# Expert down-projection weights loaded in 8 KB pieces, gate/up weight columns read with a stride of four

## The reference

```python
def swiglu(h, w_gu, w_down):
    g, u = jnp.split(h @ w_gu, 2, axis=-1)
    return (jax.nn.silu(g) * u) @ w_down

def moe_swiglu(h, router_w, router_b, w_gu, w_down):
    ...
    for e in range(N_EXPERTS):
        y = y + combine[..., e:e + 1] * swiglu(h, w_gu[e], w_down[e])
```

## Time and profile before

| | us |
|---|---|
| median of three runs (lowest, highest) | 1466.25 (1466.15, 1468.07) |
| the profiled execution, its own time | 1464.35 |
| its span in the profile | 1462.6 |

### The profile page before, as it was taken

One profiled execution on the slowest core, in us unless ns is written; L12 is line 12 of the kernel. 1 busy time (PEld: TensorE's weight loads), 2 busy tenths in 40 slices (PEclk: granted clock), 3 DMA queues, 4 the chain that ended last, 5 costly groups with the idle time before them and its releaser, 6 DMA issues.

```text
span 1462.6 us, 38889 instructions
## 1 busy us (share of the span) xinstructions
PE 1267.1 (87%) x15885; PEld 802.6 (55%) x15885; DVE 750.8 (51%) x1108; ACT 324.3 (22%) x706; POOL 42.0 (3%) x43
## 2 busy tenths in 40 slices
PE   3898998999987689979988997999899799889940
PEld 1458966888876655535544553555455355445520
DVE  0687736777754545534443543444455344435422
ACT  1105644333333311111111111111111111111110
POOL 1010000000010120000000000000000000000001
PEclk8899999999998699989999998999999899989975
DMA  9985021888898047999999999999999999999943
GB/s 339 392 329 194 2 87 32 287 291 297 298 387 327 1 165 268 393 394 375 395 393 395 395 393 394 396 394 393 395 395 393 394 379 395 393 395 395 393 160 108
DMA packets 199498, 460.71 MB, mean 315 GB/s; under 512 B 9584, under 2 KB 34848, under 8 KB 199328
## 3 DMA queue, kind: packets, MB, share of 16 engines
q1 hardware_dynamic: 185296, 403.79, 74.3%
q0 software_dynamic: 13984, 56.49, 10.4%
q10 hardware_dynamic: 192, 0.08, 0.0%
HBM read 456.66 MB, written 4.59 MB: 315 GB/s over the span
## 4 chain that ended last, share of the span: by engine, by line
issue 64%; PE 27%; DMA 4%; DVE 3%; ACT 1%; POOL 1%; POOLq 0%; SPq 0%; DVEq 0%; ACTq 0%
PE ps L801 4%; PE ps L629 3%; PE ps L757 3%; PE ps L758 3%; PE ps L759 3%; DMA ctx_tok<-in_ctx 2%; PE ps L747 2%; PE ps L689 2%; DMA ada<-in_ada_w 1%; PE ps L594 1%; PE ps L678 1%; PE ps L912 1%; PE ps L670 1%; PE ps L669 1%; PE ps L666 1%
## 5 line engine op out<-in xcount | busy, mean ns | idle before, releaser
L937 PE MATMUL ps<-w_gu,consts_sb 128*32 128x256 f32 x8960 | 539.6, 393 | 73.2 <-DMA w_gu<-in_moe_w_gu 71.4
L937 PEld LDWEIGHTS ps<-w_gu,consts_sb 128*32 128x32 f32 x8960 | 282.4, 112 | 278.0 <-DMA w_gu<-in_moe_w_gu 83.8
L1604 DVE COPY w_dn<-w_next 128x2048 f32<-128x2048 f32 x280 | 329.9, 1221 | 0.0
L949 PE MATMUL ps<-w_dn,consts_sb 128*32 128x256 f32 x4512 | 274.8, 384 | 1.6 <-DVE w_dn L1604 1.6
L949 PEld LDWEIGHTS ps<-w_dn,consts_sb 128*32 128x32 f32 x4512 | 149.6, 112 | 103.7 <-issue 10.6
L1596 DVE TENSOR_TENSOR consts_sb<-consts_sb,ps 128x128 f32<-128x128 f32 x140 | 40.4, 288 | 297.2 <-ACT consts_sb L1198 287.8
L1198 ACT ACTIVATE consts_sb<-ps 128x128 f32<-128x128 f32 x140 | 38.9, 278 | 567.9 <-PE ps L937 567.9
L1600 DVE TENSOR_TENSOR y_all<-y_all,ps 128x256 f32 x140 | 59.0, 421 | 177.8 <-PE ps L949 177.8
L1288 DVE SCALAR_TENSOR_TENSOR ada_acc<-ada,cols,ada_acc 128x512 f32<-128x512 f32 x140 | 105.0, 750 | 4.0
L1418 DVE TENSOR_TENSOR f_lo<-f_raw,f_hi 128x2048 fp32r<-128x2048 f32 x33 | 75.5, 2292 | 54.2 <-ACT f_hi L1085 52.7
L1085 ACT ACTIVATE f_hi<-f_raw 128x2048 fp32r<-128x2048 f32 x33 | 63.2, 1917 | 70.2 <-DMA f_raw<-in_ffn_w_gu 57.7
(11 more groups left out here) (218 smaller groups left out, 967.2 us busy)
## 6 DMA issues: line engine op xcount, KB each, us to landing
w_gu<-in_moe_w_gu SPq DMA_DIRECT2D x224, 1024.0 KB, 14.9
w_next<-in_moe_w_down SPq DMA_DIRECT2D x112, 1024.0 KB, 13.2
ada<-in_ada_w POOLq DMA_DIRECT2D x23, 2048.0 KB, 9.9
f_raw<-in_ffn_w_gu SPq DMA_DIRECT2D x44, 512.0 KB, 6.8
f_raw<-in_ffn_w_down SPq DMA_DIRECT2D x11, 1024.0 KB, 5.0
wqkv<-in_attn_w_qkv SPq DMA_DIRECT2D x3, 2048.0 KB, 19.4
wo_sb<-in_attn_w_o SPq DMA_DIRECT2D x1, 4096.0 KB, 23.8
y_rows<-y_all SPq DMA_DIRECT2D x80, 32.0 KB, 1.5
```

What stands on the lines that cost most here:

```text
L937: mm = pe.matmul(ps[UNIT * t:UNIT * t + UNIT, GU_BANK, 0:2 * W], x_cur[:, k, :], gate_up_columns(w_gu[x], half, kk, t), start=(k == 0), st ...
L949: mm = pe.matmul(ps[UNIT * t:UNIT * t + UNIT, Y_BANK, 0:OW], m_actT[:, q % QW, q // QW, :], w_dn[:, q, OW * t:OW * t + OW], start=(q == 0) ...
L1604: dve.tensor_copy(w_dn[:, 2 * half:2 * half + 2, :], w_next[:, y, 2 * half:2 * half + 2, :]).then_inc(s[f"d_copied{half}"], 1)
```

## The change

Each partition now holds four consecutive rows of the slice's down weights: `w_dn[p, q]` is row 4 p + q. The two rows that one transfer brings to a partition are then 8 KB in one piece. To match, column tile t takes every fourth gate and up column, starting at t: its moving operand is two runs of 128 elements that are 16 bytes apart from one to the next, where before they were adjacent. The results that leave tile t are the hidden values 4 c + t for c = 0 to 127, which after the transpose lie on partition c of chunk t.

```diff
-    mdn_v = moe_down[0].rearrange("e (q p) n -> e p q n", p=P)
+    mdn_v = moe_down[0].rearrange("e (s p q) n -> e s p q n", p=P, q=MS // P)
...
         def load_down(y, e, step):
 
             for half in range(2):
-                src = mdn_v[bass.ds(e, 1), :, bass.ds(step * (MS // P) + 2 * half, 2), :]
-                sp.dma_start(w_next[:, y, 2 * half:2 * half + 2], src.rearrange("e p k n -> p (e k) n")
+                src = mdn_v[bass.ds(e, 1), bass.ds(step, 1), :, 2 * half:2 * half + 2, :]
+                sp.dma_start(w_next[:, y, 2 * half:2 * half + 2], src.rearrange("e s p q n -> p (e s q) n")
                              ).then_inc(s[f"d_in{y}{half}"], 16)
...
     def gate_up_columns(w, half, kk, t):
-        return w[:, 2 * half:2 * half + 2, kk, W * t:W * t + W]
+        return w[:, 2 * half:2 * half + 2, kk, :].rearrange("p a (c t) -> p a t c", t=TILES)[:, :, t, :]
```

## The result

The changed kernel takes 1875.9 us (median of four, 1874.23 to 1878.3) beside 1466.2 us for the one before: ratio 1.2788, 95% interval [1.2763, 1.2813]. The forecast of 1459 was wrong in sign and size.

What follows compares the result with a forecast made beforehand. DMA's weight stream was taken to set the time from 562 to 1363.6 us. 1464.35 - 6.8 (pieces) + 0 (stride) = 1457.5, plus 1.9 for the median: 1459; range 1452 to 1885, the forecast's own 1453 to 1463.

Steps and rivals of the forecast that it cites:

- I take 0: L937's gate/up matmuls: moving elements 16 bytes apart cost nothing; bounds 0 to 3.47 us more for each unit.
- the rival: L937: each strided element is its own fetch, halving the stream; unit 9.05 us, +412 us, 1878; chance 0.26.
- The DVE reduction: Trace row on DVE: 8 elements 128 bytes apart take 165 ns, adjacent 161; a far element 1.56 ns.
- The rival's sum: L937: 138 x 9.05 = 1249 us in place of 833.3, +3.5, -6.9: +412 us, 1878.
- PE's slack: PE between 562.05 and 1395.37 us: 770 of 833.3 us needed, 63 us to give, 0.46 us each unit.
- The pieces: Down-weight loads in 8 KB instead of 4 KB pieces: 0.144 us saved a step, 7.2 us, less 0.4: -6.8 us.
- the rows: Profile rows of the weight stream's rates and piece sizes, giving 9.0 ns fixed for each piece; the skill's rule gives 3.5.

Runs made afterwards that it cites:

- the run with the slow clock: The kernel before, with short strided streams on PE, ACT and DVE after each engine's last work, PE first waiting for the stores; 1467.58 us in one run.
- the single stream: One-tile form of moving streams at several strides, added to the kernel before after PE's last work; total 1472.69 us, stride three 1.318 ns a column.

## Why the prediction was wrong

**The step that failed** is "I take 0" for the stride of four. Measured, the stride costs 3.76 us for each unit (7.23 for 3.47), and PE sets the pace from the first unit to the last. The 0 rested on two reasons, and both fell. The first: the adjacent stream follows the array's clock exactly, so the memory path is not its limit. That is true, but it bounds only what the adjacent stream asks: one group of 16 bytes in 3.42 ns, against a price of 1.76, room for a factor of 1.9. The stride asks four times as many groups. I had shown that there was room and not how much, and took it for enough. The second, that four tiles on the same 16 bytes touch no more memory together, is refuted by L995 and L998: sharing or not makes no difference (451 and 458 ns), each stream pays for itself.

**What I had kept as the rival's support pointed the right way.** The DVE reduction gave 1.56 ns for a far element, the PE path measures 1.76. That the two numbers are so near is luck: in the run with the slow clock DVE starts a product of 512 elements every 0.33 us adjacent and every 0.54 us at stride four, 1.05 ns an element and not 1.56. The Trainium skill (SBUF — State Buffer, the note on cachelines in section Door 1) says that consecutive accesses want two hits on a 16-byte line, and gives four fp32 elements as the free stride. The runs agree on the size of the line and on two hits as nearly enough (0.88 ns against 0.85), and they add the price, 1.76 ns a line. As a free stride of up to four fp32 the rule does not hold: at four the time is doubled, at three it is 54% up.

**The rival's sum.** Its mechanism and place are confirmed: L937 at 7.4 us, no waits for weights, DMA share under 1, busy time of L937 near 1000 us (1042.3). Its time of 1878 was near 1875.9 by luck. The unit was set at 9.05 us and is 9.36, mostly since the stream pays 1.76 ns and not 2 x 0.85 = 1.70, and there are 139 unit distances from 512.9 us on, of which 131 lie behind 562.05, where I had counted 138. With the right count and my unit it would have been 1464 + 139 x 9.05 - 882.5 - 7 = 1832; with the measured unit 516.1 + 139 x 9.36 = 1817.2 for the last start, and 1818.43 is measured. So the short unit took away about what the wrong count had added. The same miscount made PE's slack too small: 139 x 5.58 = 776 us of 882.5, so 0.77 us for each unit and not 0.46, or 22% of the gate/up time. The stride of four takes 3.8.

**The pieces** were sized well: one packet of 8 KB each, 1.0 us in an even round where 1.15 was worked out from the 9.0 ns of a packet, -4.8 us [-7.0, -2.6] where -6.8 was forecast. An even round has 128 packets of each engine fewer, so 1.0 to 1.1 us are 8 to 8.4 ns a packet, which speaks for the rows. By the Trainium skill (DMA: Bandwidth & Descriptors, Why small descriptors are slow), three cycles a packet make 0.45 us a round and 2.8 us in all, an estimate from its figures that lies at the interval's edge and is less than half of what an even round shows. In the changed kernel the gain is worth nothing, because DMA no longer sets the pace: 1875.9 us with the pieces, 1876.54 without.

**What remains open:** why stride three costs 346 ns in the kernel and 337 by the single stream, and why stride two adds 0.19 us to a unit where 0.13 us was expected and the streams alone give 16 x 7 ns = 0.11. In both, the kernel has more DMA traffic beside the streams than the single measurements had, but at stride four that made no difference, so it is not shown to be the cause. What inside the memory path takes the 1.76 ns the runs don't show either; they show what it depends on.

## What to carry to other kernels

A moving fp32 operand should take at least two elements from each 16 bytes; every group that is opened costs at least 1.76 ns however little is taken from it, on each stream by itself. When a resource is shown not to be the limit, ask how much more the change will demand of it, and compare that factor with the room. And before a duration is multiplied, take first start and last start from the line's own row, not from the first row of a window.

## What was not expected of the hardware

The stationary operand has about the same price. Two forms of eight weight loads of 128 columns from the run with the slow clock, in the timeline of the weight loads and at a granted clock of 1.00:

```profile
1410.14 0.97 PEld L987 LDWEIGHTS ps<-consts_sb,w_gu 128*128 128x128 f32 x8
1411.03 1.94 PEld L989 LDWEIGHTS ps<-consts_sb,w_gu 128*128 128x128 f32 x8
```

Adjacent, the eight follow each other after about 111 ns, which is also what the 128 moving columns of their matmuls take (128 x 0.85 = 109 ns). With stride four it is about 230, and 128 x 1.76 is 225. ACT nearly doubles too, DVE does not (single instructions of 512 elements: shortest/median/longest ns, first to last start in us):

```profile
L1227 ACT ACTIVATE w_gu<-w_gu x1: 622/622/622, 1405.4 to 1405.4; 128x512 f32<-128x512 f32 x1
L1231 ACT ACTIVATE w_gu<-w_gu x1: 1148/1148/1148, 1408.2 to 1408.2; 128x512 f32<-128x512 f32 x1
L1653 DVE TENSOR_SCALAR w_gu<-w_gu x1: 419/419/419, 1409.0 to 1409.0; 128x512 f32<-128x512 f32 x1
L1656 DVE TENSOR_SCALAR w_gu<-w_gu x1: 612/612/612, 1410.0 to 1410.0; 128x512 f32<-128x512 f32 x1
```

ACT goes from 622 to 1148 ns (1191 in the other of the two), and from 0.52 to 1.06 us between two starts; stride two takes 679 and 716 ns. DVE goes from 419 to 612 ns, and from 0.33 to 0.54 us between starts, which is 46% or 64% more and not the double; stride two takes 422 ns. Each of these forms was run once or twice.
